# Last pair of k tiles of each product computed row half by row half, with a token for each PSUM bank

## What is computed

```python
# first block
h = rms_norm(x, g_pre) * (1 + scale) + shift           # scale, shift, gate from silu(c) @ w_ada
proj = h @ w_in                                        # 2048 x 20032
q_mla, kv_a, z_mla, qkv_dil, z_dil, gl_mla, gl_dil = split(proj)
a  = mla_branch(q_mla, kv_a) * silu(z_mla)             # 16 heads, latent keys and values
bb = dilated_branch(qkv_dil) * silu(z_dil)             # 3 groups of 8 heads
merged = sigmoid(gl_mla) * (a @ w_mla_proj) + sigmoid(gl_dil) * (bb @ w_dil_proj)
x = x + gate * rms_norm(merged @ w_o, g_post)
# second block, two layers
y = sparse_attention(x @ w_in_a) @ w_out_a             # layer 0; layer 1: stick breaking, w_q_b, w_out_b
x = layer_norm(ALPHA * x + y)
x = x + (p[i] @ w_ple[i]) * sigmoid(x @ w_ple_gate[i])
```

## Time and profile before

| what | value |
|---|---|
| median of three runs | 2474.22 us |
| the profiled execution's own time | 2475.72 us |
| its span, first to last instruction | 2474.4 us |
| mean granted TensorE clock | 0.986 |
| DVE busy | 1496.3 us (60%) |
| ACT busy | 1133.7 us (46%) |
| POOL busy | 110.6 us (4%) |
| weights read | 458.42 MB by the queue of SyncE, 190 GB/s of all queues over the span |

### The profile page before, as it was taken

How to read it: one execution, slowest core, us unless ns; L and a number is a source line. 1 busy time by engine, 2 the same in 40 slices (tenths; PEclk the granted TensorE clock), 3 DMA queues, 4 the chain that set the end, 5 groups by cost and what they waited for, 6 DMA issues and landing times.

```text
span 2474.4 us, 28104 instructions
## 1 busy us (share of the span) xinstructions
PE 2372.7 (96%) x11204; PEld 1974.9 (80%) x11204; DVE 1496.3 (60%) x2082; ACT 1133.7 (46%) x1482; POOL 110.6 (4%) x120
## 2 busy tenths in 40 slices
PE   7899999989999999999998999999899999999988
PEld 4577888878888887888887888888788888888867
DVE  6887665444545445776755685566655456456664
ACT  4233444434444454453344444554455545455343
POOL 1000000000000000000000000000100011011010
PEclk9999999999999999999998999999899999999999
DMA  8886544535553457887564545555456555555544
GB/s 348 323 312 244 170 140 127 158 128 188 188 191 113 139 177 246 296 291 255 170 195 148 166 159 171 159 161 186 157 181 193 167 173 170 182 163 171 198 149 151
DMA packets 133542, 470.56 MB, mean 190 GB/s; under 512 B 15537, under 2 KB 15793, under 8 KB 132385
## 3 DMA queue, kind: packets, MB, share of 16 engines
q1 hardware_dynamic: 130688, 458.42, 56.4%
q0 software_dynamic: 1424, 9.37, 1.0%
q10 hardware_dynamic: 1298, 0.97, 0.1%
HBM read 466.60 MB, written 2.10 MB: 189 GB/s over the span
## 4 chain that ended last, share of the span: by engine, by line
PE 80%; DVE 6%; ACT 3%; issue 1%; DMA 1%; POOL 0%; DVEq 0%; ACTq 0%
PE G L466 24%; PE G L468 24%; PE G L467 24%; PE A L541 4%; DVE wlo L378 2%; PE A L791 1%; PE A L815 1%; ACT whi L376 1%; ACT dil L496 1%; PE A L991 1%; DMA raw<-in_weights 0%; DVE dil L1729 0%; PE A L1456 0%; DVE CP L1735 0%; PE A L957 0%
## 5 line engine op out<-in xcount | busy, mean ns | idle before, releaser
L378 DVE TENSOR_TENSOR wlo<-raw,whi 128x1024 fp32r<-128x1024 f32 (+2 forms) x782 | 937.3, 1202 | 743.3 <-ACT whi L376 740.9
L376 ACT ACTIVATE whi<-raw 128x1024 fp32r<-128x1024 f32 (+2 forms) x782 | 800.5, 1026 | 852.4 <-PE G L468 739.4
L466 PE MATMUL G<-whi,XH 128*128 128x512 f32 (+3 forms) x2804 | 1091.0, 389 | 29.7 <-DVE wlo L378 13.3
L468 PE MATMUL G<-whi,XL 128*128 128x512 f32 (+3 forms) x2804 | 1070.6, 382 | 0.0
L467 PE MATMUL G<-wlo,XH 128*128 128x512 f32 (+3 forms) x2804 | 1069.8, 382 | 0.0
L466 PEld LDWEIGHTS G<-whi,XH 128*128 128x128 f32 x2804 | 529.6, 189 | 129.3 <-DVE wlo L378 19.1
L468 PEld LDWEIGHTS G<-whi,XL 128*128 128x128 f32 x2804 | 528.8, 189 | 95.9
L467 PEld LDWEIGHTS G<-wlo,XH 128*128 128x128 f32 x2804 | 529.9, 189 | 90.5 <-issue 0.5
L328 DVE CUSTOM_DVE_ANT_0 raw<-raw,dil 128x1024 f32<-128x1024 f32 x64 | 84.9, 1339 | 10.4 <-DMA raw<-in_weights 10.4
L466 PE MATMUL A<-whi,XH 128*128 128x512 f32 x164 | 70.0, 427 | 6.3 <-DVE XL L643 3.4
L468 PE MATMUL A<-whi,XL 128*128 128x512 f32 x164 | 64.6, 394 | 0.0
(11 more groups left out here) (195 smaller groups left out, 1621.0 us busy)
## 6 DMA issues: line engine op xcount, KB each, us to landing
raw<-in_weights SPq DMA_DIRECT2D x792, 512.0 KB, 4.2
raw<-in_weights SPq DMA_DIRECT2D x80, 384.0 KB, 3.1
raw<-in_weights SPq DMA_DIRECT2D x16, 288.0 KB, 2.9
raw<-in_weights SPq DMA_DIRECT2D x8, 336.0 KB, 3.0
FT<-in_xT SPq DMA_DIRECT2D x4, 512.0 KB, 5.6
Xn<-in_x POOLq DMA_DIRECT2D x1, 2048.0 KB, 11.8
GG<-in_ln_g POOLq DMA_DIRECT2D x2, 1024.0 KB, 8.4
CP<-in_ln_b POOLq DMA_DIRECT2D x2, 1024.0 KB, 5.1
```

The source lines that it names most:

```text
L376: th = AC.mark(nc.scalar.activation(h[:, 0:2 * cols], r[:, 0:2 * cols], ACT.Copy))
L378: tl = VE.mark(nc.vector.tensor_tensor(l[:, 0:2 * cols], r[:, 0:2 * cols], h[:, 0:2 * cols].bitcast(F32), ALU.subtract))
L466: nc.tensor.matmul(o, h, wh, start=(k == start), stop=False)
L468: ins = nc.tensor.matmul(o, l, wh, start=False, stop=(k == nkt - 1))
```

## The change

In the last slot of each product the order becomes row half first, k tile second. A token is marked behind the sixth of the twelve matmuls, for bank 0, and the one behind the twelfth stands for bank 1; each bank has its own token (`pair[hf].done`), and every eviction waits for that of its bank. In the other slots order and tokens are as before, and both banks carry the slot's token. The planner's cost of a last slot is counted in two halves.

```diff
 class Bank:
     def __init__(self, t):
         self.t = t
         self.free = []
+        self.done = None
...
-            for kk in range(2):
+            last = k0 + 2 == nkt
+            for kk, hf in ((0, 0), (1, 0), (0, 1), (1, 1)) if last else ((0, 0), (0, 1), (1, 0), (1, 1)):
                 k = k0 + kk
                 PE.wait(whole_ready[k] if s in WHOLE else ready[k])
-                for hf in range(2):
-                    o = pair[hf].t[:, 0:cols]
...
+                o = pair[hf].t[:, 0:cols]
...
-            PE.busy(12 * (cols + 32) / 2400.0)
-            t = PE.mark(ins)
+                if last and (kk, hf) == (1, 0):
+                    PE.busy(6 * (cols + 32) / 2400.0)
+                    pair[0].done = PE.mark(ins)
+            PE.busy((6 if last else 12) * (cols + 32) / 2400.0)
+            t = pair[1].done = PE.mark(ins)
+            if not last:
+                pair[0].done = t
             mm_done[s] = t
...
-                    VE.wait(t, free.get(key))
+                    VE.wait(pair[hf].done, free.get(key))
...
-                tk = act_copy(buf[:, hf, 0:cols], pair[hf].t[:, 0:cols], [t, free.get(key)], func, **kw)
+                tk = act_copy(buf[:, hf, 0:cols], pair[hf].t[:, 0:cols], [pair[hf].done, free.get(key)], func, **kw)
...
-                VE.wait(t, *gl_t[0][c])
+                VE.wait(pair[hf].done, *gl_t[0][c])
...
-                ts = act_copy(sq[:, :], pair[hf].t[:, :], [t, free.get("sq")], ACT.Square,
+                ts = act_copy(sq[:, :], pair[hf].t[:, :], [pair[hf].done, free.get("sq")], ACT.Square,
...
-                    VE.wait(t)
+                    VE.wait(pair[hf].done)
```

More of the change, by code:

```diff
@@ L451, in gemm_slot @@
                     pump()
-            for kk in range(2):
+            last = k0 + 2 == nkt
+            for kk, hf in ((0, 0), (1, 0), (0, 1), (1, 1)) if last else ((0, 0), (0, 1), (1, 0), (1, 1)):
                 k = k0 + kk
                 PE.wait(whole_ready[k] if s in WHOLE else ready[k])
-                for hf in range(2):
-                    o = pair[hf].t[:, 0:cols]
[L457 to L461, removed]
+                o = pair[hf].t[:, 0:cols]
+                if s in WHOLE:
+                    ins = nc.tensor.matmul(o, FT[:, k, hf * 128:(hf + 1) * 128],
+                                           in_raw(n)[:, kk * cols:(kk + 1) * cols],
+                                           start=(k == start), stop=(k == nkt - 1))
+                else:
                     h = xh[:, k, hf * 128:(hf + 1) * 128]
@@ L713, in first_and_second_block @@
                     if g == 0:
-                        tk = act_copy(dst, src, [t, part_tok[e][hf]])
+                        tk = act_copy(dst, src, [pair[hf].done, part_tok[e][hf]])
                     else:
-                        VE.wait(t, part_tok[e][hf])
+                        VE.wait(pair[hf].done, part_tok[e][hf])
                         tk = VE.mark(nc.vector.tensor_tensor(dst, src, dst, ALU.add))
@@ L1205, in gate_chunk @@
             for hf in range(2):
-                tk = act_copy(GL[g][:, hf, 512 * c:512 * c + 512], pair[hf].t[:, :], [t, *gl_free], ACT.Sigmoid)
+                tk = act_copy(GL[g][:, hf, 512 * c:512 * c + 512], pair[hf].t[:, :], [pair[hf].done, *gl_free], ACT.Sigmoid)
                 pair[hf].free = [tk]
@@ L1303, in first_and_second_block @@
                 d1 = GL[1][:, hf, 512 * c:512 * c + 512]
-                VE.wait(t, *gl_t[1][c])
+                VE.wait(pair[hf].done, *gl_t[1][c])
                 tk = VE.mark(nc.vector.tensor_tensor(d1, pair[hf].t[:, :], d1, ALU.mult))
```

## The result

The changed kernel takes 2460.57 us (median of four runs, 2459.34 to 2461.14) beside 2474.68 us of the kernel before in the same session (four runs, 2472.71 to 2475.74). The ratio is 0.994, 95% interval 0.9927 to 0.9952. The direction was forecast; the size was not: some 14 us where the sum had 7.95, and 0.994 x 2474.22 = 2459.4 us lies just under the range.

What follows compares the result with a forecast made beforehand. PE, busy 2372.7 of 2474.4 us, was taken to set the end, so only its idle time or low clock could yield gains. Eight terms sum to 7.95 us: 2474.22 - 7.95 = 2466.3 us, range 2464.1 to 2470.0, with rivals 2460.0 to 2472.0.

Steps and rivals of the forecast that it cites:

- The eight terms: Eight places where PE waits behind an eviction, from the start to the end; gains forecast to sum to 7.95 us.
- the last query product: Layer 0: PE's 1.50 us wait shrinks through the eviction pitch and less slowing of DVE beside POOL; gain 1.40 us.
- the gate product: Last gate product but one of layer 0: PE's 0.84 us wait for the transposes goes; gain 0.84 us.
- the layer norms: Two layer norms: DVE, idle 0.34 us before, runs half 0 earlier; 0.34 us each, 0.68 us together.
- Late next behind w_o: After the product with w_o: 0.72 us off PE's 4.76 us wait, then the square root's table load is late, 1.28 us.
- The order of issue: Planner may move some ten eviction-dependent steps up a slot; effect between -4.8 and +12 us, taken as 0.
- Rival (a): Only the plain chains gain: end, w_o, gate product, layer norms, 3.58 us, giving 2470.6 us; chance 0.16.
- (b): Slower: moved-up steps put transposes ahead of their data in PE's queue, 1.2 us each, 2479.5 us; chance 0.07.
- (c): Moved steps help: four 1.2 us waits for the shared bank's copy part, 2461.5 us; chance 0.15.
- Rival (d): The token between sixth and seventh matmul holds the array: at most 1.5 us, 2467.8 us, or 2470.3 us; chance 0.05.
- I take 0 of 1.7: A 3.40 us stretch at clock 0.50 behind a shortened wait might be spared, worth up to 1.7 us; counted as 0.
- the term's 0.59: One of three evictions of the start, with DVE idle 0.74 us before: forecast gain 0.60 us.

Runs made afterwards that it cites:

- the two halves of the program: Early tokens in the old order of issue, only from about 490 us on (2465.45 us, ratio 0.9961), or only up to there (2474.93 us, 0.9999).
- the latent copies' tokens: Early tokens in the old order of issue, plus the second latent product's two copies each waiting for their own bank's token: 2462.6 us, ratio 0.9948.

## Why the prediction was right in direction and too small

**What held.** The eight terms: 7.95 forecast, 7.90 measured; that the sum agrees so closely is in part luck, since errors of up to 0.4 us cancel. The largest are the last query product (1.01 of 1.40: I had the slowing of DVE beside POOL at half of 2.18 us, and the wait kept 0.49 us) and, the other way, the gate product and the layer norms. Late next behind w_o is what I named: the wait kept 4.04 us. The order of issue, taken as 0 between -4.8 and +12 us, is 0 in the time (1.0003). Rival (a) falls, since the terms with a second step came as well; (b) and (c) fall with that order, and the four waits for the shared bank stand at 4.8 us. Rival (d) falls by the spacing of 0.22 us across the token and by stretches without a wait of a term: from 530.03 to 975.43 us of the kernel before 22 products carry the added token, and the same slots took 445.40 us there, 445.45 in the changed kernel and 445.42 with the early release alone.

The Trainium skill's page "TensorE: Matmul & The Clock Gate", section "The cost: per-tile semaphore tail", has 26.3 ns for each increment where every one of several small packed tiles makes one; the prediction carried that over to one increment in the middle of a slot. By the Trainium skill's figure the 22 tokens would cost 0.58 us, an estimate from that page. No run here shows such a price: the slots took 0.02 to 0.05 us more.

**What failed: "I take 0 of 1.7".** The low clock was the one addition that I had named, and I left it out. With it fails "the change therefore cannot make PE's own work shorter": the same instructions kept PE busy for 5.5 us less. In the start, the low stretch of the earlier trace rows stood in four of six profiles with the old release and in none of eleven with an early one; the stretch around it took 14.8 us on average and 13.1, so 1.1 us beside the term's 0.59, of which the stretch ahead of it took some 0.2 back. The low clock did not vanish there, it moved: in eight of those eleven profiles a stretch at the low clock begins between 84 and 87 us, and in none of the six, as here in the second profile of the changed kernel:

```profile
85.40:88.80 3.40, 3.40 (x9) 2.65 (x9) 3.40 (x7) 1.06 (x1) 0.00 (x0) 0.50 1.02 410
```

There DVE is busy throughout and the DMA engines for 1.02 of the time; the stretch that holds it (64.6 to 99.4 us in the kernel before) took 35.3 us on average in those eight profiles and 35.3 in the other three. So the low clock costs little in that place. Behind the key product it is 1.8 us, which I had not looked for at all: I read only the wait's own bracket, and not the clock of what follows it. That the shorter wait is the reason is argued from these averages; the one profile with early tokens only from 490 us on (46.76 us) speaks against the wait alone.

**What failed: "All other products, some 140 of 151, gain nothing."** Behind the second gate chunk PE goes on, as I said, but the queue of GpSimd does not: its load of x2 waits for that eviction. I followed each eviction to PE's next wait and not to the transfers that hang on it; 1.4 us on average by the counts, 1.8 by the stretch. And behind three earlier query products of layer 0 the next slot began 0.24 us sooner each, 0.7 us. At the first of them the four transposes ahead of it start at 1504.87 us and the slot's first matmul at 1505.47 before, 0.60 us later; after, 1493.49 and 1493.84, 0.35 us. Before, that matmul waits for the split, as behind the last query product, but for so short a time that the wait has no bracket in the timeline and was not on my list.

By the prediction's own sign, "a gain that comes from other places than these", it was wrong: some 5 us did. Together: 7.9 + 0.9 + 1.8 + 1.4 + 0.7 = 12.7 of the 13.5 us that the release alone gives (13.1 with 1.8 for the load). The rest is within what the low clock at other waits differs by from profile to profile (PE was busy for 36 to 46 us at the low level in profiles of the two kernels). Open remains why the kernel with only the gate chunk late lost nothing in time, and how the shares split exactly: the two halves of the program do not add up to the whole, though their intervals leave room for it.

## What to carry to other kernels

Releasing a bank half a slot early is worth the pitch of two evictions where one engine stays busy, and the whole half slot where the chain behind it is idle; both can be read from the brackets, here to 0.2 us for each place but the last query product, where a second engine is at work (0.39 us). Then look past the wait: at the granted clock of the matmuls behind it, and at every queue (GpSimd's above all) that waits for the same eviction. Where PE must stand still ahead of much work, move what it waits for behind other work, or give it something harmless to do: here these two, with the latent copies' tokens (a wait 0.37 us shorter), gave 11.5 us on top of the release's 13.5, most of it by moving the wait for p.

## What the runs showed of the hardware

The same attention stretch, with the same work and the same waits ahead of it, took from 42.91 to 46.76 us in nine profiles, with PE's granted clock between 0.96 and 0.85. The part of the gain that is clock has to be counted over many profiles; of the 47 waits above 0.3 us themselves 39 agreed to 0.02 us between the two profiles of the kernel before.

A transfer of 2 MB, issued 0.49 us earlier against the stream of the weights, landed after 9.4 to 10.0 us every time, and after 8.9 to 9.1 or 11.7 to 11.8 us where it was issued later: two ways, with nothing between.
